# Choosing the first four experts' rows by a shortcut, signalled and selected tile by tile into six PSUM banks

## What is computed

```python
g_logits = hf @ w_rg + b_rg                       # 4 groups
grp = argmax(g_logits)
e_logits = (hf @ w_re + b_re)[..., grp]           # 8 experts of the group
top_val, top_idx = lax.top_k(e_logits, 2)
eid = grp * 8 + top_idx                           # 2 experts per token
# the assignments are sorted by expert, and each expert e does for its rows
y = (silu(x @ w_gate[e]) * (x @ w_up[e])) @ w_down[e]
```

## Time and profile before

| | us |
|---|---|
| median of 3 runs | 1873.34 (1871.31 to 1874.74) |
| the profiled execution | 1869.85 |
| its span | 1868.0 |
| mean granted clock of the tensor engine | 0.983 |

### The profile page before, as it was taken

How to read it: one execution, slowest core, us unless ns; L and a number is a source line. 1 busy time by engine, 2 the same in 40 slices (tenths; PEclk the granted TensorE clock), 3 DMA queues, 4 the chain that set the end, 5 groups by cost and what they waited for, 6 DMA issues and landing times. The chain is left out here.

```text
span 1868.0 us, 27615 instructions
## 1 busy us (share of the span) xinstructions
PE 1750.6 (94%) x11702; PEld 1335.4 (71%) x11702; DVE 808.3 (43%) x1403; ACT 592.6 (32%) x1007; POOL 60.3 (3%) x86
## 2 busy tenths in 40 slices
PE   6999989899999989979999998999999999999997
PEld 2884444666666556538856787899998799999886
DVE  3864655411111111234377576352246545444333
ACT  4333432100000000036577434453323333222222
POOL 1001000000000000020000000000000000000000
PEclk9999989999999999999999999899999999999999
DMA  9855633799999999972110111122223032233321
GB/s 370 272 195 161 272 105 115 278 427 427 426 427 427 426 426 427 427 291 67 58 46 8 40 46 46 46 91 91 91 97 107 12 113 91 91 101 103 102 79 45
DMA packets 110630, 348.87 MB, mean 187 GB/s; under 512 B 8587, under 2 KB 71329, under 8 KB 97191
## 3 DMA queue, kind: packets, MB, share of 16 engines
q1 hardware_dynamic: 105910, 337.59, 47.3%
q0 software_dynamic: 4224, 9.31, 1.4%
q10 hardware_dynamic: 370, 0.14, 0.0%
HBM read 323.92 MB, written 23.07 MB: 186 GB/s over the span
## 5 line engine op out<-in xcount | busy, mean ns | idle before, releaser
L1785 PE MATMUL psum<-parts_memory 128*128 128x256 f32 (+3 forms) x1088 | 332.0, 305 | 18.7 <-DVE linear_memory L1817 5.3
L1786 PE MATMUL psum<-parts_memory 128*128 128x256 f32 (+3 forms) x1088 | 327.9, 301 | 0.0
L1787 PE MATMUL psum<-parts_memory 128*128 128x256 f32 (+3 forms) x1088 | 327.9, 301 | 0.0
L1684 DVE TENSOR_TENSOR parts_memory<-fixed,parts_memory 128x1024 fp32r<-128x1024 f32 x139 | 166.9, 1221 | 207.1 <-ACT parts_memory L1676 206.6
L1785 PEld LDWEIGHTS psum<-parts_memory 128*128 128x128 f32 x1088 | 207.3, 191 | 31.2 <-issue 12.5
L1786 PEld LDWEIGHTS psum<-parts_memory 128*128 128x128 f32 x1088 | 207.4, 191 | 6.8
L1787 PEld LDWEIGHTS psum<-parts_memory 128*128 128x128 f32 x1088 | 207.1, 190 | 6.9
L1785 PE MATMUL psum<-mix_parts,parts_memory 128*128 128x256 f32 (+2 forms) x664 | 206.0, 310 | 2.7 <-PEq L2890 2.0
L1786 PE MATMUL psum<-mix_parts,parts_memory 128*128 128x256 f32 (+2 forms) x664 | 206.7, 311 | 0.0
L1787 PE MATMUL psum<-mix_parts,parts_memory 128*128 128x256 f32 (+2 forms) x664 | 206.1, 310 | 0.0
L1676 ACT ACTIVATE parts_memory<-fixed 128x1024 fp32r<-128x1024 f32 x139 | 143.2, 1055 | 112.4 <-PE psum L1787 109.6
(11 more groups left out here) (459 smaller groups left out, 2417.5 us busy)
## 6 DMA issues: line engine op xcount, KB each, us to landing
fixed<-in_w_exp_gate_dram SPq DMA_DIRECT2D x19, 2048.0 KB, 26.2
fixed<-in_w_exp_up_dram SPq DMA_DIRECT2D x19, 2048.0 KB, 23.6
fixed<-in_w_in_dram SPq DMA_DIRECT2D x36, 1024.0 KB, 8.6
fixed<-in_w_exp_down_dram SPq DMA_DIRECT2D x18, 2048.0 KB, 28.3
attention_memory<-in_w_exp_down_dram SPq DMA_DIRECT2D x14, 2048.0 KB, 25.8
attention_memory<-in_w_exp_up_dram SPq DMA_DIRECT2D x13, 2048.0 KB, 28.9
attention_memory<-in_w_exp_gate_dram SPq DMA_DIRECT2D x13, 2048.0 KB, 26.2
fixed<-in_w_mod_dram SPq DMA_DIRECT2D x8, 2048.0 KB, 9.1
```

Of the source, the lines that this page charges most:

```text
L1684: dve.tensor_tensor(out, raw, high.bitcast(F32), ALU.subtract).then_inc(self.low_ok, 1)
L1785: pe.matmul(out, x(0), w(0), start=start, stop=False)
L1786: pe.matmul(out, x(0), w(1), start=False, stop=False)
L1787: return pe.matmul(out, x(1), w(0), start=False, stop=stop)
```

## The change

The first batch's places come from a shortcut: expert number times 64, plus the rank, plus 1024 (outside of the batch) where the rank is 64 or more. It needs the ranks but not the counts and the swap. The tiles are signalled one by one (`first_ok`), and the tensor engine selects tile by tile: three pairs into banks 0 to 5, and then the fourth pair with all four tiles into bank 6. The planner's chain runs behind the choices, and shifts `place` by one batch itself, so that `pick_ok` counts from the second batch on. Two idle products instead of four stand behind the rank matmuls. `last_route_pe` moves behind the first expert's gate and up and half a selection, and the end of the vector routing (`last_route_dve`) behind the first expert's output.

```diff
+    first_base, first_rank, first_over = room(2 * TT), room(2 * TT), room(2 * TT)
+    g["first_place"] = first_place = room(2 * TT)
...
         pe.matmul(psum[:, 7, P:P + EXPERTS], ones, earlier[:, TT - 1, :], start=False, stop=True).then_inc(rank_ps, 1)
-        idle_products(g, pe, 0, 4)
+        idle_products(g, pe, 0, 2)
...
+        dve.tensor_scalar(ngm, gmax[:, :, 0], -1.0, None, ALU.mult).then_inc(neg_ok, 1)
+        dve.tensor_tensor(gap, emax[:, :, 1], emax[:, :, 0], ALU.subtract).then_inc(gap_ok, 1)
+        step(dve.tensor_scalar(by_choice(first_base), chosen.rearrange("p t k -> p k t"), float(BR), None, ALU.mult))
         dve.wait_ge(rank_ps, 1)
         ranks = psum[:, 7, 0:P].rearrange("p (t n) -> p t n", t=TT)
+        step(dve.tensor_tensor(flat_choices(picked), flat_choices(hot), psum[:, 7, 0:P].unsqueeze(1).to_broadcast([P, 2, TT * EXPERTS]),
+                               ALU.mult))
+        step(dve.tensor_reduce(first_rank, picked.rearrange("p k t n -> p (k t) n"), AX_X, ALU.add))
+        step(dve.tensor_scalar(first_over, first_rank, BR - 0.5, float(BC * BATCH), ALU.is_ge, ALU.mult))
+        step(dve.tensor_tensor(first_base, first_base, first_rank, ALU.add))
+        step(dve.tensor_tensor(first_place, first_base, first_over, ALU.add))
+        choose_first_rows()
+
         step(dve.tensor_copy(counts, psum[:, 7, P:P + EXPERTS]))
...
         step(dve.tensor_reduce(place, picked.rearrange("p k t n -> p (k t) n"), AX_X, ALU.add))
-        by_choice = lambda x: x.rearrange("p (k t) -> p k t", k=2)
-        choose_rows()
+        step(dve.tensor_scalar(place, place, -float(BC), None, ALU.add))
...
-        dve.tensor_scalar(ngm, gmax[:, :, 0], -1.0, None, ALU.mult).then_inc(neg_ok, 1)
-        dve.tensor_tensor(gap, emax[:, :, 1], emax[:, :, 0], ALU.subtract).then_inc(gap_ok, 1)
...
+    def last_route_dve(dve):
+        step = Steps(dve, late_step)
         dve.wait_ge(row_ps, 1)
...
                 if s % PAIRS == 0 and part == 0:
-                    pe.wait_ge(pick_ok, s // PAIRS + 1)
+                    pe.wait_ge(pick_ok, s // PAIRS)
...
+            def select_first():
+
+                def part_of_tile(u, part, t, bank, lo):
+                    for i in range(2):
+                        last = pe.matmul(psum[:, bank, lo:lo + BC], h2P[:, i, t, (2 * u + part) * P:(2 * u + part + 1) * P], pick[:, t, :],
+                                         start=(t == 0 and i == 0), stop=(t == TT - 1 and i == 1))
+                    return last
+
+                for t in range(TT):
+                    pe.wait_ge(first_ok, t + 1)
+                    for u in range(PAIRS - 1):
+                        for part in range(2):
+                            last = part_of_tile(u, part, t, 2 * u + part, 0)
+                        if t == TT - 1:
+                            last.then_inc(x_ps, 1)
+                for part in range(2):
+                    for t in range(TT):
+                        last = part_of_tile(PAIRS - 1, part, t, 6, part * BC)
+                last.then_inc(x_ps, 1)
+
             route_pe(pe)
-            pe.wait_ge(pick_ok, 1)
-            for u in range(PAIRS):
-                select(u, u, 0)
-                select(u, u, 1)
-            last_route_pe(pe)
+            select_first()
...
                 if b < EXPERTS:
                     select_next(b, 0)
+                if b == 0:
+                    last_route_pe(pe)
                 turn_h(b)
...
+                if isinstance(s, int) and s < PAIRS - 1:
+                    x = psum[:, 2 * u:2 * u + 2, 0:BC]
+                else:
+                    x = psum[:, 6 if isinstance(s, int) and s < PAIRS else BX + u % 2, :].rearrange("p (k n) -> p k n", k=2)
+                act.activation(xT[:, i, 2 * u:2 * u + 2, :], x, ACT.Copy).then_inc(xt_ok, 1)
...
-            route_dve(dve, lambda: choose_rows(0))
+            def choose_first_rows():
+
+                for t in range(TT):
+                    step(first_choice(t, first_place))
+                    second_choice(t, first_place).then_inc(first_ok, 1)
+
+            route_dve(dve, choose_first_rows)
...
                 take_y(b)
+                if b == 0:
+                    last_route_dve(dve)
```

More of the change, by code:

```diff
@@ L927, in output_and_routing @@
     h2s, h2_high, h2_low = sem("h2_ready"), sem("h2_high_parts"), sem("h2_low_parts")
-    dstep = sem("routing_dve_step")
+    dstep, late_step = sem("routing_dve_step"), sem("late_routing_step")
     t_ps, t_sb = sem("h2T_in_psum"), sem("h2T_ready")
@@ L1048, in route_act, with route_dve @@
         act.activation(gap_exp, gap, ACT.Exp).then_inc(gap_exp_ok, 1)
-    def route_dve(dve, choose_rows):
+    def route_dve(dve, choose_first_rows):
         step = Steps(dve, dstep)
@@ L1142, in route_dve @@
         low_rows(TT - 1)
+        by_tile = lambda x: x.unsqueeze(1).to_broadcast([P, TT, EXPERTS])
+        by_choice = lambda x: x.rearrange("p (k t) -> p k t", k=2)
+        flat_choices = lambda x: x.rearrange("p k t n -> p k (t n)")
+        dve.tensor_scalar(ngm, gmax[:, :, 0], -1.0, None, ALU.mult).then_inc(neg_ok, 1)
+        dve.tensor_tensor(gap, emax[:, :, 1], emax[:, :, 0], ALU.subtract).then_inc(gap_ok, 1)
+        step(dve.tensor_scalar(by_choice(first_base), chosen.rearrange("p t k -> p k t"), float(BR), None, ALU.mult))
         dve.wait_ge(rank_ps, 1)
         ranks = psum[:, 7, 0:P].rearrange("p (t n) -> p t n", t=TT)
+        step(dve.tensor_tensor(flat_choices(picked), flat_choices(hot), psum[:, 7, 0:P].unsqueeze(1).to_broadcast([P, 2, TT * EXPERTS]),
[5 more added lines that the diff above has]
+        choose_first_rows()
         step(dve.tensor_copy(counts, psum[:, 7, P:P + EXPERTS]))
@@ L1162, in route_dve @@
         step(dve.tensor_scalar(shift, shift, float((FIRST_MORE - 1) * BR), None, ALU.add))
-        by_tile = lambda x: x.unsqueeze(1).to_broadcast([P, TT, EXPERTS])
         step(dve.scalar_tensor_tensor(out=where, in0=by_tile(is_twin), scalar=-float(BR), in1=ranks, op0=ALU.mult, op1=ALU.add))
@@ L1204, in route_dve @@
         dve.tensor_tensor(wt[:, :, 1], wt[:, :, 0], gap_exp, ALU.mult).then_inc(routed, 1)
-    return route_sync, route_pool, route_pe, last_route_pe, route_act, route_dve, routed
+    return route_sync, route_pool, route_pe, last_route_pe, route_act, route_dve, last_route_dve, routed
 EXPERT_SLOTS = 7
@@ L1301, in experts @@
         g["used_ok"], g["order_ok"] = used_ok, order_ok
-        route_sync, route_pool, route_pe, last_route_pe, route_act, route_dve, routed = output_and_routing(g, sem, dma_sem)
+        route_sync, route_pool, route_pe, last_route_pe, route_act, route_dve, last_route_dve, routed = output_and_routing(
+            g, sem, dma_sem)
         expert_of, order, more, place, iota, h2P = g["expert_of"], g["order"], g["more"], g["place"], g["iota"], g["h2P"]
+        first_place, first_ok = g["first_place"], sem("first_rows_chosen")
         g["y_sb"], g["w_read"] = y_sb, w_read
@@ L1445, in more_rows @@
                 where = [(slot, i * 16 + 16 * uses) for slot, uses in zip(MORE_SLOTS, MORE_USES)]
-                pe.wait_ge(pick_ok, batch + 1)
+                pe.wait_ge(pick_ok, batch)
                 for u in range(PAIRS):
@@ L1480, in take_x @@
                 act.wait_ge(x_ps, s + 1)
-                act.activation(xT[:, i, 2 * u:2 * u + 2, :], psum[:, BX + u % 2, :].rearrange("p (k n) -> p k n", k=2),
-                               ACT.Copy).then_inc(xt_ok, 1)
+                if isinstance(s, int) and s < PAIRS - 1:
[3 more added lines that the diff above has]
+                act.activation(xT[:, i, 2 * u:2 * u + 2, :], x, ACT.Copy).then_inc(xt_ok, 1)
             def gate(b):
@@ L1517, in _, with first_choice, second_choice @@
             step = Steps(dve, picked_step)
-            def first_choice(t):
+            def first_choice(t, place=place):
                 return dve.tensor_scalar(found[:, t % 2, :], iota, place[:, t:t + 1], None, ALU.is_equal)
-            def second_choice(t):
+            def second_choice(t, place=place):
                 return dve.scalar_tensor_tensor(out=pick[:, t, :], in0=iota, scalar=place[:, TT + t:TT + t + 1],
@@ L1532, in choose_rows @@
                 second_choice(TT - 1).then_inc(pick_ok, 1)
-                dve.wait_ge(pick_ok, batch + 1)
+                dve.wait_ge(pick_ok, batch)
                 step(dve.tensor_scalar(place, place, -float(BC if batch < EXPERTS // BATCH else BR), None, ALU.add))
```

## The result

The changed kernel takes 1860.82 us, the median of eleven runs (1853.71 to 1866.34); eleven runs of the kernel before, taken beside them, have a median of 1873.18 (1870.69 to 1875.28). The ratio is 0.9942, with a 95% interval of 0.9927 to 0.9958: faster by 12.4 us. The profiled execution took 1860.82 us with a span of 1859.1, against 1869.85 and 1868.0.

A forecast was written before the change was run, and what follows sets the result against it. Bound: the experts' saturated DMA stream, held by the serial path to the eighth load. Selection start 6.83 plus clock 1.47 gives 8.3 us, less 0.4 at the tenth load: 7.9, so 1873.34 becomes 1865.4 us; range 1862.5 to 1871.0.

The forecast's parts named there:

- The bound and the mechanism: Experts' saturated weight stream: it ends earlier only if it starts earlier, at the eighth load, 352.35 to 344.05 us.
- Start of the selection: Tensor engine: first tile ready by 331.34, idle products end at 331.84 and set the start, 6.83 us earlier than 338.67.
- Selection: 64 matmuls at 0.12 us each, 7.64 us; 1.47 us gained because the clock stays up.
- Tiles: Vector engine: later tiles' choices come every 0.78 us, or every 0.91 with no overlap.
- Banks: Selection writing six banks in turn: taken as zero cost; upper bound 0.26 us at 24 changes, 6.2 us.
- both rivals: Bank changes drain for 6.2 us: at full clock gain 1.7 (5 in 100), or with half clock 1879.3 us (4 in 100).
- The next choice: Next batch's choice, signalled at 347.5 against a need at 347.39: tensor engine waits about 0.2 us in the first expert.
- the step behind it: Tenth load issued 7.9 us earlier, not 8.3; the 0.4 us counts because the stream isn't full there.
- The end of the routing: Routing matmul L1022 moves from the last copy's shadow into the first expert's chain: 0.20 us.
- What lies behind the tenth load: Full stream, combine and second block: start on the experts' results and move as a body, nothing added.
- Rival three: Behind the earlier stream start the time is given back, by half-clock stretches or uneven stream pace: near 1871 us, 6 in 100.
- The base and the spread: Starting median 1873.34 us less 7.9; the range allows the runs' spread of 1.7 us each way.

The follow-up runs named there:

- delayed: The changed kernel with nine idle products between the last copy of the selected rows and the first gate projection; ratio 0.9989 against the kernel before.
- ranks filled: The changed kernel with two more idle products ahead of the rank matmuls; ratio 0.9945 against the kernel before.
- old order: The changed kernel, shortcut kept, first batch selected after one wait for all four tiles, pair by pair into two banks; ratio 0.9968 against the kernel before.
- all tiles: The changed kernel with one wait for all four tiles, then the new order into six banks; ratio 0.9969 against the kernel before.

## Why the prediction was right and wrong

**The bound and the mechanism: right.** The experts' stage ends with its DMA stream, and the stream moves as a body with its eighth load. That is shown, not only argued: by the table, by the delay put into the kernel before, and by the delay put into the changed one.

**Start of the selection: the vector chain right, "the idle products, and not the vector engine, set the start" wrong.** I had the first tile ready for the engine at 3.15 us behind the last rank matmul (331.34 from 328.19) and the idle products done at 3.65 (331.84), and took the later. The first matmul starts at 3.17 to 3.20 in the five executions, at 3.17 with no idle products and at 3.22 where the engine waits 1.03 us for the tile: it starts on the tile. What the two products do is to hold back the second matmul, whose weight load is issued 0.38 to 0.82 us behind the first one's, against 0.16 with no idle products. So their 0.5 us were not in the start but in the length of the selection. With four products the start does move, to 4.75 us.

**Selection: 0.9 us too short.** 7.64 us forecast; 7.93 and 7.94 at full clock, and in the five executions of the changed kernel 8.21, 8.23, 8.32, 8.89 and 9.26, 8.58 in the mean. Two things were missing: the idle products' rest at its start, and the clock, which came back 3.1, 3.2, 3.4, 4.6 and 5.5 us behind the last rank matmul. I had taken the moment of its return from one trace as fixed (331.5, 3.3 us behind); the executions differ in it. That the sum came out is luck in part, since the errors of the two steps largely offset each other: from the last rank matmul to the eighth load 15.86 us were forecast (344.05 less 328.19), 16.17 is the measured mean.

**Tiles: right.** The second tile's choice starts 0.79 us after the first's (330.01, 330.80), for which I had 0.78. Where the vector engine waits for its own results the pair takes 0.91. The section "The DRAIN you can't avoid" of the Trainium skill's page VectorE: DVE Perf Modes says that one can't skip the wait between two operations by leaving out semaphores; here the two times differ by 0.12 us, and the trace doesn't agree. The same section does say, which I had left out, that a next operation that is not held starts earlier.

**Banks: right, both rivals fall.** 7.96 against 7.98 us. The Trainium skill's page TensorE: Matmul & The Clock Gate, section "A second HAM failure mode: psum-queue depth-cycling", speaks of a clock that swings when matmuls go round the banks, in another kernel, with 512 columns in bf16. Here, with 256 columns in split floats, the clock stays at 1.00 from 333 us to the end of the selection, and the trace doesn't show it.

**The next choice: small, as forecast, but the step behind it failed.** The next choice ends at 347.14 and its matmuls start at 347.60, so nothing waits for it in the profiled execution; in an execution whose eighth load comes earlier (+15.78) the engine waits 0.21 us for it, and in the earliest (+15.56) 0.51. The tenth load is 0.27 us less early than the eighth (7.71 against 7.98; 0.4 forecast). I wrote "It counts, because the stream isn't full yet there". It doesn't show: from eighth load to first gather the stretch is 0.4 us *shorter* than before (458.2 against 458.6 in the means). The gap behind the tenth load is in both kernels (347 GB/s in 355 to 360 us, 380 in 360 to 365 before), and 0.27 us more of lateness leave no trace at the stream's end. Why not isn't shown.

**The end of the routing: right in the sum, its worth not seen.** "+0.2 us" was the matmul's own duration, and that is what it takes where it now stands (0.20 at 348.75). But I had called the move small. What the move does is to keep the tensor engine from waiting 2.4 to 2.9 us for the planner's chain, and from the lower clock behind that wait: 5 us. I had the time at which the planner's column is ready in my own sum, but asked only what the moved matmul costs where it now stands, not what it would cost where it had stood.

**What lies behind the tenth load: a term set to zero.** 7.9 forecast against 7.71 measured is right. But all that lies behind it was taken as "should move as a body", and it gave another 2.2 us (9.9 less 7.7), with an error of near 1. Some 0.6 us of it are in the stream and the step to the combine, 1.7 in what follows. Single runs do say that the changed kernel spends less time at the lower clock, 60.2 ± 1.6 us against 67.3 ± 0.6, and within each kernel a microsecond at the lower clock goes with 0.37 us of time, which makes 2.6 us; at equal time at the lower clock the kernels would be 7 us apart. But the five profiles of each don't show where: 61.0 us against 63.3 in all, with 1.6 less in the routing (5.9 against 7.5) and 1.4 less in 1200 to 1600 us, the latter from a single execution. The variants don't settle it. Where the engine waits 1.03 us or not at all ahead of the selection (four idle products, delayed, ranks filled), single runs spend 59.5, 61.3 and 56.1 us at the lower clock and gain 1.4 to 2.2 us more than their eighth load is earlier. With waits of 1.3 to 2.6 us there (old order, all tiles, no idle products) they spend 67.1, 64.8 and 66.7 and gain nothing more. But the runs without the shortcut and with the routing's end put back gain 1.7 and 2.1 us more at 68.1 and 66.4, and each of these gains has an error of about 1 us. So about a fifth of the gain lies behind the tenth load, measured to 1 us, and its cause stays open. Rival three expected time to be given back behind the start; if anything is there, it has the other sign.

**The base and the spread: the failed step of the sum, which put the time out of the range.** From 1873.34 I subtracted 7.9 and allowed "the runs' spread of 1.7 us each way", half the width of three runs. The single runs of one kernel spread over 14 to 16 us, so the mean of three runs has an error of 1.7 us by itself, and that of eleven about 1. The median of the three lay 2.8 us above the mean of 152. From 1870.6 the same working gives 1862.7, and the range moved down likewise, 1859.7 to 1868.2, holds 1860.82, though only 1.1 us above its low end: the 2.2 us set to zero are missing there too. Between the forecast of 1865.4 and the measured 1860.82 lie 4.6 us: 2.8 of them are the base and 2.2 what lies behind the tenth load, less 0.2 that the forecast had too much for the mechanism and 0.2 by which this median lies above the changed kernel's mean. Of the 12.4 us in the first comparison 2.6 are this offset of before, 7.7 the mechanism and 2.2 what lies behind it (12.5, rounding included).

## What to carry to other kernels

At the head of a saturated DMA stream, price a change by the time to the first slot that it frees, and expect that time at the end one to one, in either direction (here to within about 2 us, for shifts from 8.6 us earlier to 3.7 later). When a stage is filled up to raise the clock, look for what else it waits for once it runs faster: here a copy that stood behind other work on the scalar engine. Compare executions from an event that both share and that lies right ahead of the change, not by their spans, and take the spread of the base from stages that the change doesn't touch or from many runs, never from three. When a stage is made earlier, ask of each step left in place what it now waits for: on the tensor engine a wait of 2 to 3 us was paid once as a wait and once more as work at the lower clock.

## What the runs showed of the hardware

- Executions whose code is the same up to the last rank matmul started that matmul between 322.0 and 330.0 us, with 0 to 23.9 us at the lower clock ahead of it. The DMA-bound part doesn't spread so: the 448 us from the tenth load to the first gather varied by 2.7 us over twenty executions of twelve kernels.
- After a wait of 2.92 us the clock was granted at 0.50 for the next stretch of work (344 to 345 us above), though the matmuls ahead of the wait had run at full clock. After waits of 1.33 and 1.70 us ahead of the selection (old order, all tiles) the selection ran at 1.00.
- Filler work isn't free of the clock that it should raise: nine idle products took 10.06 us behind the rank matmuls, where the clock was at its lower level at first, and 7.99 behind the selection.
- 64 matmuls of 128x256 took 7.93 us when 48 of them changed their bank after every two, and 7.94 when they changed it after every sixteen.
